# The gated delta rule's stage reordered: projections of values, gates and memory stand between the steps of its inverse

## The reference, cut to what matters

```
h = rms_norm(x, norm_mix_w[0])
proj = h @ gdn_w_in[0]                     # q, k, v, z: 8 heads x 128 each, b, a: 8 each; then memory queries 4 x 128
qkv = silu(causal_dwconv(cols[..., :3 * wd], conv_w))       # 4 taps
beta, g = sigmoid(b), -exp(a_log) * softplus(a + dt_bias)
o = gated_delta_rule_chunked(l2norm(q), l2norm(k), v, g, beta)
mix = rms_norm(o, norm_w) * silu(z)
mo = memory_attention(qm, rms_norm(mem), mem_w_kv[0])       # 256 memory tokens, 4 heads, softmax
x = x + concat([mix, mo]) @ w_out[0]
x = x + conv_glu(rms_norm(x, ...), ...)
```

## Time and profile before

| what | value |
|---|---|
| median of 3 runs | 2741.77 us |
| the profiled execution | 2738.46 us |
| its span in the profile, first to last instruction | 2736.6 us |
| PE busy over the span | 2502.0 us (91%) |
| DVE, ACT, POOL busy | 894.9, 522.6, 52.0 us |
| mean granted TensorE clock | 0.964 |

### The profile page before, as it was taken

One profiled execution on the slowest core, in us unless ns is written; L12 is line 12 of the kernel. 1 busy time (PEld: TensorE's weight loads), 2 busy tenths in 40 slices (PEclk: granted clock), 3 DMA queues, 4 the chain that ended last, 5 costly groups with the idle time before them and its releaser, 6 DMA issues.

```text
span 2736.6 us, 28361 instructions
## 1 busy us (share of the span) xinstructions
PE 2502.0 (91%) x11512; PEld 1632.2 (60%) x11512; DVE 894.9 (33%) x2139; ACT 522.6 (19%) x1149; POOL 52.0 (2%) x79
## 2 busy tenths in 40 slices
PE   8989699999999999998878999999898879999997
PEld 6879558856875885577644444444676544444443
DVE  4366428431142754335331111111443331111112
ACT  2132311001252100214321111111324221111111
POOL 0000000000100000002000000000020000000000
PEclk9989899999999999999989999999999989999999
DMA  8310056674722777443128999999442149999995
GB/s 310 108 62 1 1 185 243 244 283 147 223 93 89 273 263 272 167 149 98 56 98 369 397 412 415 414 416 413 169 154 93 62 162 415 417 419 419 390 415 243
DMA packets 148880, 653.81 MB, mean 239 GB/s; under 512 B 14538, under 2 KB 20938, under 8 KB 124032
## 3 DMA queue, kind: packets, MB, share of 16 engines
q1 hardware_dynamic: 145600, 642.98, 60.0%
q0 software_dynamic: 3136, 8.86, 1.3%
HBM read 648.67 MB, written 3.15 MB: 238 GB/s over the span
## 4 chain that ended last, share of the span: by engine, by line
PE 84%; DVE 9%; issue 3%; ACT 2%; DMA 1%; SPq 1%; DVEq 0%; ACTq 0%
PE ps L106 82%; DVE AR L125 3%; PE ps L109 3%; ACT AR L115 1%; DVE AR L120 1%; SPq L101 1%; DMA wring<-in_ffn_w_up 1%; DVE SM L137 0%; DVE AR L133 0%; DVE AR L129 0%; DVE X L125 0%; DVE SM L145 0%; DVE AR L121 0%; ACT L115 0%; ACT SM L115 0%
## 5 line engine op out<-in xcount | busy, mean ns | idle before, releaser
L106 PE MATMUL ps<-wring,AR 128*64 128x512 f32 (+3 forms) x3776 | 928.5, 586 | 55.8 <-issue 48.0
L106 PE MATMUL ps<-HT,wring 128*128 128x256 f32 x3200 | 727.2, 389 | 1.6 <-DMA wring<-in_gdn_w_in 1.4
L106 PEld LDWEIGHTS ps<-wring,AR 128*64 128x64 f32 (+2 forms) x3776 | 372.5, 146 | 579.2 <-issue 573.7
L106 PEld LDWEIGHTS ps<-HT,wring 128*128 128x128 f32 x3200 | 622.9, 196 | 98.1 <-issue 6.8
L115 ACT ACTIVATE AR<-ps 128x512 f32<-128x512 f32 (+6 forms) x274 | 138.4, 505 | 1038.6 <-PE ps L106 583.0
L106 PE MATMUL ps<-AR 128*128 128x128 f32 (+6 forms) x1288 | 284.4, 370 | 26.4 <-DVE AR L125 16.4
L125 DVE TENSOR_TENSOR AR<-ps,AR 128x512 f32<-128x512 f32 (+2 forms) x120 | 67.1, 559 | 655.9 <-PE ps L106 651.2
L106 PEld LDWEIGHTS ps<-AR 128*128 128x128 f32 (+4 forms) x1288 | 178.0, 191 | 121.5 <-issue 82.0
L106 PE MATMUL ps<-AR,XN 128*128 128x128 f32 x1024 | 124.2, 281 | 4.5 <-DVE AR L125 4.5
L129 DVE SCALAR_TENSOR_TENSOR wring<-wring,CC 128x512 f32<-128x512 f32 x168 | 126.3, 752 | 6.0
L109 PE MATMUL ps<-CS,AR 128*128 128x128 f32 (+2 forms) x474 | 80.9, 293 | 51.1 <-DVE AR L120 25.8
(11 more groups left out here) (149 smaller groups left out, 1353.6 us busy)
## 6 DMA issues: line engine op xcount, KB each, us to landing
wring<-in_w_gate SPq DMA_DIRECT2D x64, 2048.0 KB, 13.6
wring<-in_w_up SPq DMA_DIRECT2D x64, 2048.0 KB, 9.7
wring<-in_w_down SPq DMA_DIRECT2D x64, 2048.0 KB, 12.2
wring<-in_w_ada SPq DMA_DIRECT2D x24, 2048.0 KB, 12.1
wring<-in_ffn_w_up SPq DMA_DIRECT2D x20, 2048.0 KB, 10.3
wring<-in_w_in SPq DMA_DIRECT2D x18, 2048.0 KB, 7.5
wring<-in_w_out SPq DMA_DIRECT2D x10, 2048.0 KB, 7.7
wring<-in_ffn_w_down SPq DMA_DIRECT2D x10, 2048.0 KB, 12.7
```

Of the source, the lines that this page charges most:

```text
L106: return Ins(self.eng and self.eng.matmul(out, lhs, rhs, start=start, stop=stop), None)
```

## The change

What is computed stays the same. In the first block: x is loaded in halves, the identity ahead of the vectors; of the nine small loads two stay on SP (one behind chunk 0, with the gate rows) and seven move to GpSimd's queue, behind the last qkv product. On PE the gate columns follow chunk 0; cumsum and decays go between chunks 2 and 4 (decays to PA banks); key norms, in pairs, follow chunk 4; the products of quarters 0 and 2 come before chunk 5, those of 1 and 3 within it. The first level takes the quarters in the order 0, 2, 1, 3. Memory's features and first keys and the turns of values follow; the rest of memory's keys and values, qm and z are computed in halves of chunks behind levels 1 to 5. Memory's heads run between the state's steps, from level 6 on. The out projection begins with memory's chunk and turns the outputs into CAT between its parts. The scaling of values and keys and the copies of memory's queries move from VectorE to ScalarE. Tiles move so that this is possible: values into CAT, KD behind the levels' tiles (32 columns more of SBUF), ST into XN, memory's scores into HT. SP's fills follow the new order, with one slot deferred. The diff, cut to its core ("..." for what is left out; the new helpers `conv`, `decay`, `products`, `first_level`, `queries` and the like hold the operations of the old loops):

```diff
     CAT = at(0, 12, 256)
-    QK, ab, VB = at(3072, 16, 256), at(7168, 2, 16), at(7200, 8, 256)
-    RN, RN1, RN2 = at(9248, 256), at(9504, 256), at(9760, 256)
+    QK, ab, VB = at(3072, 16, 256), at(7168, 2, 16), CAT[:, 0:8, :]
+    RN, RN1, RN2 = (XF[:, 256 * j:256 * j + 256] for j in range(3))
     D, DT, LT, BT = ([at(7200 + 2048 * i + 512 * j, 4, 128) for j in range(4)] for i in range(4))
     AT = [four(MF[:, 512 * j:512 * j + 512]) for j in range(4)]
-    KD = HT[:, 0:4, :].rearrange("p a b -> p (a b)")
-    ST = HT[:, 4:8, :].rearrange("p a b -> p (a b)")
+    KD, ST = at(15392, 1024), XF[:, 0:1024]
     SQ = Ring([XF[:, 256 * j:256 * j + 256] for j in range(8)])
-    G = at(ARENA - 22 * 256, 22, 256)
+    G = at(10752, 22, 256)
...
+        if tag == ("mem", 0):
+            return (ring((tag, "s"), lambda: [HT[:, 2 * j:2 * j + 2, :] for j in range(3)]),
+                    ring((tag, "t"), lambda: [HT[:, 6:8, :]]))
+        base = 6192 if tag[0] == "mem" else 12832
...
-        x, c, c1, c2 = dma("x"), dma("c"), dma("c1"), dma("c2")
-        e.dma_start(X[:, :, :], t["x"][0].rearrange("(a p) d -> p a d", p=128)).then_inc(x)
+        c, c1, c2 = dma("c"), dma("c1"), dma("c2")
+        for m in range(2):
+            e.dma_start(X[:, m, :], t["x"][0, 128 * m:128 * m + 128, :]).then_inc(dma(f"x{m}"))
+        e.dma_start(CS[:, 0:128], t["cst"][:, 0:128]).then_inc(c)
         e.dma_start(PV[:, :], t["vecs"]).then_inc(c)
-        e.dma_start(CS[:, 0:128], t["cst"][:, 0:128]).then_inc(c)
         gw = t["gdn_w_in"][0]
-        weights(("qkv", 0), gw[:, 0:512], 8, 512)
+        qkv = lambda chunk: weights(("qkv", chunk), gw[:, chunk * 512:chunk * 512 + 512], 8, 512)
+        qkv(0)
+        e.dma_start(SW[:, :, 0:16], gw[:, 4096:4112].rearrange("(k p) n -> p k n", p=128)).then_inc(c2)
+        e.dma_start(RB[:, :], t["rows"].broadcast_to([128, nrow])).then_inc(c2)
+        qkv(1)
         e.dma_start(CS[:, 128:ncst], t["cst"][:, 128:ncst]).then_inc(c1)
-        e.dma_start(RB[:, :], t["rows"].broadcast_to([128, nrow])).then_inc(c2)
-        rows = lambda src: src.rearrange("(k p) n -> p k n", p=128)
-        successive = lambda src: src.rearrange("(p k) n -> p k n", p=128)
-        e.dma_start(SW[:, :, 0:16], rows(gw[:, 4096:4112])).then_inc(c2)
-        e.dma_start(SW[:, :, 16:40], rows(t["nsa_w_in"][0, :, 2560:2584])).then_inc(c2)
-        for l in range(2):
-            o = 40 + 52 * l
-            e.dma_start(SW[:, :, o:o + 16], rows(t["w_in_2"][l, :, 2048:2064])).then_inc(c2)
-            e.dma_start(SW[:, :, o + 16:o + 20], successive(t["w_router_group_2"][l])).then_inc(c2)
-            e.dma_start(SW[:, :, o + 20:o + 52], successive(t["w_router_expert_2"][l])).then_inc(c2)
-        for chunk in range(1, 6):
-            weights(("qkv", chunk), gw[:, chunk * 512:chunk * 512 + 512], 8, 512)
-        for chunk in range(2):
-            weights(("z", chunk), gw[:, 3072 + chunk * 512:3584 + chunk * 512], 8, 512)
-        weights(("qm", 0), gw[:, 4112:4624], 8, 512)
+        for chunk in range(2, 6):
+            qkv(chunk)
         memory(0)
         memory_kv(0)
-        project("out0", t["w_out"][0], 3)
+        weights(("qm", 0), gw[:, 4112:4624], 8, 512)
+        weights(("z", 0), gw[:, 3072:3584], 8, 512)
+        W.defer()
+        weights(("z", 1), gw[:, 3584:4096], 8, 512)
+        for c in (2, 0, 1):
+            project("out0", t["w_out"][0], c + 1, c)
         ffn(0)
...
+        def column_pair(name, p, tag=None):
+
+            ps = bank(e, PB, (name, p))
+            wt = weights(name, 8, 512)
...
+            if p:
+                W.free(name, (sig("gdn_mm"), (name, p)))
 
...
+            for chunk in range(4):
+                for p in range(2):
+                    column_pair(("qkv", chunk), p, "gdn")
+                if chunk == 0:
+                    e.wait_ge(dma("c2"), END)
+                    tokens(done, "ab", SW[:, :, 0:16], 8, HT, 16)
+                else:
+                    sums(chunk - 1)
+                if chunk == 2:
...
+                    decay(0)
+                    decay(1)
+            decay(2)
+            PA.defer()
+            decay(3)
+            column_pair(("qkv", 4), 0)
+            sums(3)
+            column_pair(("qkv", 4), 1)
...
+            products(0)
+            products(2)
+            column_pair(("qkv", 5), 0)
+            turned_products(0)
+            turned_products(2)
+            products(1)
+            products(3)
+            column_pair(("qkv", 5), 1)
+            turned_products(1)
+            turned_products(3)
+            memory_features(0)
+            memory_kv(0, 0)
+            for hd in range(8):
+                ps = bank(e, PB, ("vb", hd))
+                e.wait_ge(act, ("silu", 16 + hd))
+                for m in range(2):
+                    e.transpose(ps[:, m * 128:m * 128 + 128], VB[:, hd, tok(m)], IDENT)
+                e.transpose(ps[:, 256:384], QK[:, 8 + hd, 0:128], IDENT).then_inc(done, ("vb", hd))
+
+            def fill(s):
+
+                if s == 1:
+                    memory_kv(0, 1)
+                    memory_kv(0, 2)
+                elif s == 2:
+                    memory_kv(0, 3)
+                    column_pair(("qm", 0), 0)
+                elif s == 3:
+                    column_pair(("qm", 0), 1)
+                    column_pair(("z", 0), 0)
+                elif s == 4:
+                    column_pair(("z", 0), 1)
+                    column_pair(("z", 1), 0)
+                elif s == 5:
+                    column_pair(("z", 1), 1)
+
             for s in range(1, 7):
-                for q in range(4):
+                for q in (QUARTERS if s == 1 else range(4)):
                     ps = bank(e, PB, ("inv", s, q))
                     e.wait_ge(vect, ("level", s, q))
                     for j in range(4):
                         ins = e.matmul(ps[:, j * 128:j * 128 + 128], BT[q][:, j, :], D[q][:, j, :], True, True)
                     ins.then_inc(done, ("inv", s, q))
-                for q in range(4):
+                if s == 6:
+                    for hd in range(2):
+                        memory_step(0, "scores", hd)
+                for q in (QUARTERS if s == 1 else range(4)):
                     ps = bank(e, PB, ("invt", s, q))
                     e.wait_ge(act, ("inv", s, q))
                     for j in range(4):
...
                     ins.then_inc(done, ("invt", s, q))
-
...
+                fill(s)
+
...
+            new_values(0)
+            new_values(1)
+            memory_step(0, "turned", 0)
+            memory_step(0, "scores", 2)
+            state(0)
+            state(1)
+            memory_step(0, "turned", 1)
+            memory_step(0, "out", 0)
+            from_state(0)
+            from_state(1)
+            output(0)
+            output(1)
+            memory_step(0, "scores", 3)
+            new_values(2)
+            new_values(3)
+            memory_step(0, "turned", 2)
+            memory_step(0, "out", 1)
+            output(2)
+            output(3)
+            memory_step(0, "turned", 3)
+            memory_step(0, "out", 2)
+            memory_step(0, "out", 3)
+
...
+                order, ready = (2, 0, 1), [mem, (sig("gdn_v"), ("cat", 2)), (sig("gdn_v"), ("cat", 3))]
+                halfway, between = (lambda: into_cat(0)), (lambda: into_cat(1))
+            down(sig("out_mm"), ("out", layer), [((f"out{layer}", c), 4 * c, 4) for c in order], CAT, [between], ("ffn", layer), ready, halfway)
 
...
...
+            conv(16)
+            v.wait_ge(mm, ("sum", 15))
...
+            root_inverse("rn", RN[0:16, :], done)
+            conv(17)
+            root_step("rn", RN[0:16, :], RN1[0:16, :], RN2[0:16, :], act, done, "rn")
+            for q in range(2, 4):
+                causal(q)
+            conv(18)
+            for h in range(2):
+                scaled_keys(h)
+            conv(19)
+            for h in range(2, 4):
+                scaled_keys(h)
...
+            products(0)
+            products(2)
+            memory_norm(0)
+            conv(20)
+            conv(21)
+            first_level(0)
+            first_level(2)
+            products(1)
+            products(3)
+            conv(22)
+            conv(23)
+            first_level(1)
+            first_level(3)
...
+            memory_step(0, "norm", 0)
+            memory_step(0, "scores", 2)
+            state(0)
+            state(1)
+            memory_step(0, "norm", 1)
+            from_state(0)
+            from_state(1)
+            memory_step(0, "out", 0)
+            output(0)
+            output(1)
+            memory_step(0, "norm", 2)
+            memory_step(0, "scores", 3)
+            memory_step(0, "out", 1)
+            memory_step(0, "norm", 3)
+            output(2)
+            output(3)
+            gated(0)
+            memory_step(0, "out", 2)
+            memory_step(0, "out", 3)
             gated(1)
...
...
-            memory_squares(0)
...
```

(105 more changed lines are left out.)

414 lines of the change are left out of this document (203 added, 211 removed).

## The result

Four runs of the changed kernel took 2718.03 us in the median (2715.15 to 2722.22), the kernel before 2740.14 (four runs); the ratio is 0.9922 with a 95% interval of 0.9904 to 0.9939. The forecast was 2717 with a range of 2702 to 2731 and 0.91 on faster. The profiled execution took 2719.05 us, with a span of 2717.2 us.

The account below looks back on a forecast made before the run. TensorE (PE) was taken to bound the stage, with 58 of 335.2 us lost. The stage's end moves from 391.5 to 368.1, 23.4 saved: 2715.1 from the profiled execution, 2718.4 from the median; forecast 2717 us, range 2702 to 2731.

Parts of the forecast that it names:

- The pool: First stage to the out projection: 335.2 us less 277 of PE work leaves 58 lost, 43.4 idle, about 15 low clock.
- Chunks 0 to 3: First projections with gate columns, sums, cumsum and decays: 70.0 us plus 1.1 of low clock; PE reaches chunk 4 at 84.1.
- To the first level: Chunk 4 to level 1's second half: 76 us, 14.6 of them idle, plus 3 for the clock; reached at 163.1.
- The levels: Moved work fills the gaps behind levels 1 to 5, hiding about 5 us; level 6 begins at 277.7.
- The tail: Level 6 to the out projection: 42.6 us, 11.8 idle, plus 2.1 of slow products; out projection starts at 322.4.
- The out projection: 42.3 us as before plus turns 1.9, last CAT write 0.5, slow clock 1.0: 45.7, ending at 368.1.
- Behind it: From the out projection's end to the kernel's end: the same 2345 us, starting 23.4 earlier.
- Slower, by the clock: Rival: values' turns and waits before level 1 leave TensorE slow through the levels; 2767 with two levels; chance 0.04.
- signs of being wrong: Idle between levels, clock under 0.95 within, out projection after 340, later stage giving time back, longer VectorE operations while POOL issues.
- Does not do what it says: Rival: fills hide only level gaps, other waits move at whole size; 5 to 6 us saved less 1, 2737; chance 0.05.
- Small: Rival: the stage's middle and tail come out slower than chained; 10 us saved, 2730; chance 0.14.
- large gain: Rival: evacuations overlap better and clocks stay up; 35 us saved, 2705; chance 0.16.

Follow-up runs that it names:

- levels alone: Changed kernel with all moved projections ahead of level 1 instead of behind levels 1 to 5; stage ends at 379.07 us, changed kernel 371.24.
- scaling on VectorE: Changed kernel with the 24 scalings of values and keys back on VectorE; stage ends at 370.62 us, changed kernel 371.24.
- norms over 128 rows: Changed kernel with the eight key norms as products over 128 rows instead of 16; stage ends at 372.43 us, changed kernel 371.24.
- values in levels: Changed kernel with values' turns and ScalarE's copies behind levels 1 and 2 instead of ahead of level 1; stage ends at 366.67 us, changed kernel 371.24.
- heads behind: Changed kernel with memory's four heads pipelined behind state and outputs instead of between their steps; stage ends at 380.01 us, changed kernel 371.24.

## Why the prediction was right, point by point

- **The pool.** 58 us were said to be lost, 277 us of PE work to stay. The changed kernel needs 311.7 us from its first projection to the out projection, without the turns into CAT (1.9): 36.6 us are lost against 275.1, where the forecast's own times (322.4 - 13.0) leave 34.3. The list of the 277 leaves out level 1's first 24 products (2.84 us at 211.66) and counts the full length of rows that overlap by 0.1 to 0.2 us; the two work against each other.
- **Start.** 13.0 forecast, 13.10 measured. The forecast put the lateness of chunk 1 down to the small loads; but their move wasn't needed, since with them ahead of it, on SP, the chunk came in time too, as the gate columns stand first. That X in halves gives the 0.9 us wasn't tried alone.
- **Chunks 0 to 3.** 84.1 forecast, 84.69 measured. The clock behind the gate columns cost 1.7 and not 1.1.
- **To the first level.** The chain on VectorE came as worked out: 0.39 us of waiting for the norms (0.2 forecast), 1.09 and 1.27 ahead of the last turns (0.7 and 1.3), 2.71 for memory's second bank (2.6), 2.94 for its features (3.2). Two terms were off. The clock was put at 3 us, with bounds of 0 and 6; measured against the full clock, the rows from the norms to the end of level 1 are 8 us longer: 3.3 at the 16-row norms and the products behind them, which no step foresaw (they covered a wait of 1.3), 0.3 and 1.6 at memory's turns and first keys, 0.7 at the values' turns, 2.15 in level 1. And the idle time was put at 14.6 (the waits named add up to 14.4), while 12.0 were measured: the wait at the values' turns was put at 5.2, and PE waits 0.36 to 0.71 a head there, 2.9 in all. So level 1 ended at 173.2, where the forecast has 163.1 + 7.3 = 170.4.
- **The levels.** No gap, 10.88 a level; "about 5 us" was 4.7 by the levels alone. From the end of level 1 to level 6 it takes 105.0 us, 107.3 forecast: the forecast added up the lengths of rows (10.96 for a level), but each row begins before the end of the last is over (197.70 - 186.98 = 10.72). So level 6 starts at 278.17, 277.7 forecast, because 2.8 us too many ahead of it and 2.3 too few here cancel: luck, and not a proof of either term.
- **The tail.** 44.7 forecast, 46.6 measured. The idle time was near (11.8 and 13.0), but one wait was put in the wrong place: not at "turned 2" behind norm 2 (3.4 forecast, none there), but at new values 3 (0.8 forecast), 2.44 for the bank of output 0. The forecast had followed each engine's order and in this place forgot the ring of four banks.
- **The out projection.** 45.7 forecast, 46.5 measured, with its first group at 8.80 for 7.03, 1.8 of slow clock for the 1.0 assumed.
- **Behind it.** "The same 2345 us" held in the profiled execution (2346), but this term varies by 14 us from one execution to the next with the same code, more than any other in the sum. That the median came within 1 us of the forecast is in part luck. Of the 14 us between the longest (scaling on VectorE) and the shortest (norms over 128 rows) 11.6 are PE's busy time for the same work.
- **The rivals.** *Slower, by the clock:* only level 1 ran slow, 13.03 for 10.88 (clock 0.53 from 160 to 165 us, behind the values' turns with their waits), and the levels behind it at 1.00. The rule on transposes in the Trainium skill ("TensorE: Matmul & The Clock Gate", the part on the PE-mode transpose) speaks of this place. Where level 1 followed memory's keys with no turns between, it ran at 10.88 from the start; since the waits went with the turns, that run doesn't tell the two apart. Turns alone were not enough here: the 16 back to back at 118.68, and the twelve behind level 1 in "values in levels", with a wait of 1.15 among them, were followed by the clock at 1.00. Of the signs of being wrong one came true, and only for level 1: a clock under 0.95 within the levels (0.83 from 160.3 to 173.2). *Does not do what it says:* refuted by the 20.3 us themselves; the heads behind (8.8 us) and the levels alone (7.8) show where they come from. *Small* and *large gain:* 20.3 us in the stage lie between them.

Of these 20.3 us the runs show 8.8 for memory's heads between the steps of the state and 7.8 for the projections between the levels (4.7 of it the gaps; 1.5 is the tail's clock, which may not belong to them). About 4 are left for the start, the gate columns ahead of chunk 1 and the order of products before level 1; these weren't tried one by one, and the parts need not add up exactly.

## What to carry to other kernels

Price a reordering by the lists of what each engine does in turn, and by the ring of buffers with them: the one wait that was put in the wrong place here was a bank held by a copy two steps back. Work put into the gaps of a dense loop wins little more than these gaps (4.7 us of idle time in 65 here, 7.8 with all that came with them); the same trick in a sparse chain, where one engine waits for two others, won more with less work. Add up starts and not lengths where a profile's rows overlap. And compare small edits by where the steps of the stage stand: they repeated to about 1 us here, where the whole time varies by 10 or more.

## What was not expected of the hardware

Products that use only 16 of the 128 rows let TensorE's clock fall to its lower level though the engine had no wait over 0.4 us: 0.50 from 104 to 110 us, and the next 32 products took 5.2 to 6.8 us in ten executions (in two of them behind a wait of 1.4); over 128 rows, where the others meet zeros of the identity, the clock stayed at 1.00 and they took 3.81 in three. And the same work behind this stage took 2337 to 2351 us in fourteen profiled executions; the mean clock in it was 0.96 or 0.97 throughout, most of the difference is PE's busy time, and what makes it stays open.
